# Hybrid encoder: token factors from the features-first input, and the pooled branch kept features-first

## The reference

```python
def rmsnorm(x, g):
    xf = x.astype(jnp.float32)
    y = xf * lax.rsqrt(jnp.mean(xf * xf, axis=-1, keepdims=True) + EPS)
    return (y * g.astype(jnp.float32)).astype(x.dtype)
...
        h = rmsnorm(x, norm1_g[l])
        z = jnp.matmul(h, w_in[l])
        u = z[..., :o1]
        qk = jax.nn.silu(centred_dwconv(z[..., o1:o3], conv_w[l], conv_b[l]))
...
        y_pool = pool_mixer(u, pool_w[l], pool_scale[l]).astype(x.dtype)
        y_mlstm = mlstm_mixer(q, k, v, o, gates, gate_b[l], mh_norm_g[l]).astype(x.dtype)
        x = x + jnp.matmul(jnp.concatenate([y_pool, y_mlstm], axis=-1), w_out[l])
        x = x + expert_choice_ffn(rmsnorm(x, norm2_g[l]), w_router[l], w_gate[l], w_up[l], w_down[l])
    return rmsnorm(x, final_g)[:, N_META:]
```

## Time and profile before

| | |
|---|---|
| median of 3 runs | 1764.13 us (1763.55 to 1764.77) |
| profiled execution | 1767.92 us, span 1766.1 us |
| granted TensorE clock, mean | 0.995 |
| busy share of the span | PE 98%, ACT 22%, DVE 24%, POOL 17% |
| first stage (to the last gate rows) | about 75 us of the span |
| output stage, with the ranking | about 655 to 846 us |
| experts' stage | about 854 us to the end |

### The profile page before, as it was taken

The page is one execution under the profiler, slowest core; times in us unless marked ns, Lnnn a source line. Parts: engine busy times, 40 slices in busy tenths (PEclk is TensorE's granted clock), DMA queues, the critical chain, the costliest instruction groups (busy, mean ns, idle before and its releaser), DMA issues.

```text
span 1766.1 us, 25121 instructions
## 1 busy us (share of the span) xinstructions
PE 1735.0 (98%) x10359; PEld 1403.2 (79%) x10359; DVE 420.5 (24%) x987; ACT 383.8 (22%) x890; POOL 298.4 (17%) x330
## 2 busy tenths in 40 slices
PE   9999999999999999999999999999999999999996
PEld 5556556855555774555899999999999999999996
DVE  4562113621020560069201101011010110101105
ACT  3335224332131533455000000000000000000005
POOL 0080022520101253443000010100101001010010
PEclk9999999999999999999999999999999999999998
DMA  9211012321110535534577676876859758587585
GB/s 297 78 51 52 20 36 76 90 89 36 36 39 18 163 101 182 177 99 154 197 251 278 214 250 232 294 250 211 279 205 310 261 187 283 212 307 255 181 278 227
DMA packets 178721, 307.28 MB, mean 174 GB/s; under 512 B 11068, under 2 KB 63468, under 8 KB 178528
## 3 DMA queue, kind: packets, MB, share of 16 engines
q1 hardware_dynamic: 171408, 283.30, 46.5%
q0 software_dynamic: 7248, 23.09, 5.2%
HBM read 275.02 MB, written 31.35 MB: 173 GB/s over the span
## 4 chain that ended last, share of the span: by engine, by line
PE 95%; ACT 1%; DVE 1%; DMA 1%; issue 1%; SPq 0%; POOL 0%; DVEq 0%; ACTq 0%; POOLq 0%
PE bank L2118 32%; PE bank L2138 16%; PE bank L1890 12%; PE bank L1867 9%; PE bank L2019 8%; PE bank L1801 3%; PE bank L1837 2%; PE bank L1953 2%; PE bank L1934 1%; PE bank L1849 1%; PE bank L1846 1%; PE bank L1845 1%; PE bank L2162 1%; PE bank L2093 1%; PE bank L1972 1%; PE bank L1943 1%
## 5 line engine op out<-in xcount | busy, mean ns | idle before, releaser
L2118 PE MATMUL bank<-arena 128*128 128x164 f32 x4096 | 579.7, 303 | 0.3 <-DVE arena L1658 0.3
L2118 PEld LDWEIGHTS bank<-arena 128*128 128x128 f32 x4096 | 571.8, 190 | 0.5 <-DVE arena L1658 0.5
L2138 PE MATMUL bank<-arena 128*128 128x164 f32 x2048 | 296.4, 303 | 0.4 <-DVE arena L1669 0.4
L2138 PEld LDWEIGHTS bank<-arena 128*128 128x128 f32 x2048 | 286.7, 190 | 0.6 <-DVE arena L1669 0.6
L1890 PE MATMUL bank<-arena 128*128 128x512 f32 (+1 forms) x576 | 214.0, 534 | 0.0
L1890 PEld LDWEIGHTS bank<-arena 128*128 128x128 f32 x576 | 110.0, 191 | 102.5 <-issue 92.7
L1669 DVE TENSOR_TENSOR arena<-bank,arena 128x328 f32<-128x328 f32 x64 | 32.0, 500 | 655.8 <-ACT arena L1241 655.8
L821 POOL DMA_INDIRECT residual<-arena,cur_scatter x30 | 44.9, 1497 | 691.3 <-DVE arena L1678 633.8
L1867 PE MATMUL bank<-arena 128*128 128x384 f32 x480 | 155.7, 485 | 0.0
L1241 ACT ACTIVATE arena<-bank 128x328 f32<-128x328 f32 x64 | 28.4, 443 | 558.5 <-PE bank L2118 558.5
L2019 PE MATMUL bank<-arena 128*128 128x512 f32 x320 | 146.0, 599 | 0.8 <-issue 0.8
(11 more groups left out here) (273 smaller groups left out, 1504.2 us busy)
## 6 DMA issues: line engine op xcount, KB each, us to landing
arena<-in_w_up SPq DMA_DIRECT2D x32, 2048.0 KB, 14.7
arena<-in_w_down SPq DMA_DIRECT2D x32, 2048.0 KB, 10.3
arena<-in_w_gate SPq DMA_DIRECT2D x32, 2048.0 KB, 8.3
arena<-in_w_in SPq DMA_DIRECT2D x7, 1536.0 KB, 6.5
arena<-in_x_sample SPq DMA_DIRECT2D x14, 512.0 KB, 5.9
arena<-x_features_first SPq DMA_DIRECT2D x11, 512.0 KB, 7.8
arena<-decay_rows SPq DMA_DIRECT2D x22, 256.0 KB, 4.6
arena<-state_rows SPq DMA_DIRECT2D x44, 128.0 KB, 4.0
```

What stands on the lines that cost most here:

```text
L2118: last = pe.matmul(ps[2 * w + fp % 2][:, a * SLOTS:(a + 1) * SLOTS], ring[2 * (fp // 2) + w][:, k, f * P:(f + 1) * P], xeT[:, k, SIDE[side ...
L2138: last = pe.matmul(to, ring[4 + dp // 2][:, k, dt * P:(dt + 1) * P], hidT[:, k, :], start=k == 0, stop=k == KT - 1)
```

## The change

It has two parts.

**Token factors.** The rows are no longer loaded in the first stage. ScalarE squares the whole tile of features (1024 columns, into `sq`). For the first tile TensorE adds up over features and blocks with eight products with ones. For the ten others GpSimd first adds the eight blocks in three steps of 512, 256 and 128 columns, and TensorE does one product with ones. ScalarE takes the root of the mean of all 128 by 128 values from the bank (`factor`, in `arena`), VectorE the reciprocal of all of them, and its eight products then read both the features and the factor from SBUF, each raising `h_ready` by itself. TensorE waits block by block for the first two tiles of `output_gate`, and for all eight blocks of a tile from the third on.

**Pooled branch.** The pooled product is formed features first, stored as `pool_features`, and loaded per tile by a new `load_pool` (256 features by 128 tokens) into the first 256 columns of `y_t`. Those two blocks need no transpose; `project` reads them directly. Several groups of `warm` are shorter or gone.

```diff
-        xin = [area("kT", D, shift=(1 + i) * D) for i in range(3)] + [area("qT", D, shift=i * D) for i in range(2)]
-        xin += [area("Cb", D, shift=i * D) for i in range(6)]
         ones = area("kT", P)
-        diag = [area("kT", P, shift=(1 + s) * P) for s in range(2)]
+        factor = [area("kT", P, shift=(1 + s) * P) for s in range(2)]
+        sq = [area("kT", D, shift=(1 + s) * D) for s in range(2)]
...
-            sp.dma_start(y_t[n % 2], y_d[i * P:(i + 1) * P, :]).then_inc(y_in[n % 2], 16)
+            sp.dma_start(y_t[n % 2][:, D_POOL:Y_W], y_d[i * P:(i + 1) * P, :]).then_inc(y_in[n % 2], 16)
+
+        def load_pool(sp, n):
+
+            if n >= 2:
+                multiplied(sp, ("wo", n - 2, 1))
+            pooled = y_t[n % 2][:, 0:D_POOL].rearrange("p (j t) -> p j t", j=2)
+            sp.dma_start(pooled, pool_d.rearrange("(j p) t -> p j t", p=P)[:, :, tile_cols(ORDER_B[n])]).then_inc(y_in[n % 2], 16)
...
-                    for p0, src in x_rows[i]:
-                        sp.dma_start(xin[i][p0:p0 + src.shape[0], :], src).then_inc(x_in[i], 16)
                     sp.dma_start(hT[:, :, tile_cols(i)], x_flipped.rearrange("p (k t) -> p k t", k=KT)[:, :, tile_cols(i)]).then_inc(tile_in[i], 16)
...
                         load_y(sp, n + 2)
                         load_x3(sp, n + 2)
+                        load_pool(sp, n + 2)
...
+                for i in range(1, NT):
+                    pool.wait_ge(sq_done, i + 1)
+                    for w in (512, 256):
+                        st.do(pool.tensor_tensor(sq[i % 2][:, 0:w], sq[i % 2][:, 0:w], sq[i % 2][:, w:2 * w], ALU.add))
+                        st.settle()
+                    pool.tensor_tensor(sq[i % 2][:, 0:P], sq[i % 2][:, 0:P], sq[i % 2][:, P:2 * P], ALU.add).then_inc(sum_ready, 1)
...
-                    act.wait_ge(x_in[tile], 16 * len(x_rows[tile]))
-                    st.settle()
-                    st.do(act.activation(area("scratch", D), xin[tile], ACT.Square, accum_out=small[:, i:i + 1]))
-                    st.settle()
-                    act.activation(small[:, 32 + i:33 + i], small[:, i:i + 1], ACT.Sqrt, scale=1.0 / D, bias=small[:, 94:95]).then_inc(sq_done, 1)
+                    act.wait_ge(tile_in[tile], 16)
+                    act.activation(sq[i % 2].rearrange("p (k t) -> p k t", k=KT), hT[:, :, tile_cols(tile)], ACT.Square).then_inc(sq_done, 1)
                     if i > 1:
                         take_o(i - 2)
+                        act.wait_ge(h_ready, KT * (i - 1))
+                    multiplied(act, ("x", i))
+                    b = plan[("x", i)][0]
+                    act.activation(factor[i % 2], ps[b][:, 0:P], ACT.Sqrt, scale=1.0 / D, bias=small[:, 94:95]).then_inc(free[b], 1)
...
-                    dve.tensor_scalar(diag[i % 2], ident[:, :], small[:, 48 + i:49 + i], None, ALU.mult).then_inc(diag_ready, 1)
...
-                        st.do(dve.scalar_tensor_tensor(h, h, g1c[:, k:k + 1], ps[b][:, 0:P], ALU.mult, ALU.mult))
...
+                    st.do(dve.reciprocal(factor[i % 2], factor[i % 2]))
...
+                        dve.scalar_tensor_tensor(h, h, g1c[:, k:k + 1], factor[i % 2], ALU.mult, ALU.mult).then_inc(h_ready, 1)
...
-                    pe.wait_ge(diag_ready, i + 1)
                     b = bank(("x", i))
-                    pe.matmul(ps[b][:, 0:P], ones, diag[i % 2], start=True, stop=True).then_inc(full[b], 1)
+                    if i == 0:
+                        pe.wait_ge(zeroed, 1)
+                        pe.wait_ge(sq_done, 1)
+                        for k in range(KT):
+                            last = pe.matmul(ps[b][:, 0:P], ones, sq[0][:, k * P:(k + 1) * P], start=k == 0, stop=k == KT - 1)
+                    else:
+                        pe.wait_ge(sum_ready, i)
+                        last = pe.matmul(ps[b][:, 0:P], ones, sq[i % 2][:, 0:P], start=True, stop=True)
+                    last.then_inc(full[b], 1)
...
-                    pe.wait_ge(h_ready, i + 1)
+                    if i > 1:
+                        pe.wait_ge(h_ready, KT * (i + 1))
...
-                                    for a in range(4 * g, min(4 * g + 4, NT)):
-                                        c = (a - 4 * g) * P
-                                        last = pe.matmul(ps[b][:, c:c + P], src[:, tile_cols(a)], pw[:, j, :], start=True, stop=True)
-                                    last.then_inc(full[b], 1)
+                                    lo, hi = 512 * g, min(512 * g + 512, T)
+                                    pe.matmul(ps[b][:, 0:hi - lo], pw[:, j, :], src[:, lo:hi], start=True, stop=True).then_inc(full[b], 1)
...
-                        for k in range(4):
+                        for k in range(D_POOL // P if name == "yT" and h == 0 else 0, 4):
                             last = pe.transpose(ps[b][:, k * P:(k + 1) * P], source(4 * h + k), ident[:, :])
...
-                    pe.wait_ge(y_in[n % 2], 16 * (n // 2 + 1))
+                    pe.wait_ge(y_in[n % 2], 32 * (n // 2 + 1))
```

More of the change, by code:

```diff
@@ L1102, in _, with move @@
                         last_norm(p)
-                def move(key, out, parts=P, w=512):
+                def move(key, out, parts=P, w=512, at=0):
                     multiplied(act, key)
-                    act.activation(out, ps[plan[key][0]][0:parts, 0:w], ACT.Copy).then_inc(free[plan[key][0]], 1)
+                    act.activation(out, ps[plan[key][0]][0:parts, at:w], ACT.Copy).then_inc(free[plan[key][0]], 1)
                 def halves(name, n, slots):
                     for h in range(2):
-                        move((name, n, h), slots[n % 2][:, 512 * h:512 * h + 512])
+                        lo = D_POOL if name == "yT" and h == 0 else 512 * h
+                        move((name, n, h), slots[n % 2][:, lo:512 * h + 512], at=lo - 512 * h)
                 def exponentials(part):
@@ L1826, in _ @@
                 gate_rows(NT - 2)
-                warm(3, 5)
                 gate_rows(NT - 1)
@@ L1870, in gate_columns @@
                 def gate_columns():
-                    warm(6, 5)
                     pe.wait_ge(rows_ready, 1)
```

46 lines of the change are left out of this document (18 added, 28 removed).

## The result

| | median | runs | profiled execution | span | mean granted clock |
|---|---|---|---|---|---|
| before | 1764.45 us | 1763.55 to 1767.82 (4) | 1767.92 | 1766.1 | 0.995 |
| changed | 1789.2 us | 1787.16 to 1792.05 (4) | 1789.83 | 1788.0 | 0.992 |

The changed kernel is slower: ratio 1.0133, 95% interval 1.012 to 1.0146. The medians differ by 24.75, the two profiled executions by 21.9. The forecast was 1778.5 with a range up to 1784, so the side was right and the size was not.

The account below looks back on a forecast made before the run. TensorE was taken as the bound, 95% of the chain. Start, eight-tile chain, transposes and pooled load summed as 1764.1 - 0.5 + 11.5 - 1.7 + 5.1 = 1778.5 us; range 1768 to 1784, by its own bounds 1775 to 1784.

Parts of the forecast that it names:

- the meeting on SBUF: First stage: GpSimd's three additions push themselves between VectorE's eight scalings, both in SBUF; stall of 1.3 to 1.9 per tile.
- the late load: Output stage: tile 9's pooled load, issued at about 790.86, lands at about 795.3, after TensorE wants it: +4.7.
- the start of the stage: First stage's start: fewer bytes ahead of the weights, more work for the first tile; -0.5, bounds -1.2 and +0.3.
- the chain of eight tiles: First stage, tiles 2 to 9: root, reciprocal and stretched scalings delay output_gate; 8 x 1.44 = +11.5, bounds 10.4 to 15.2.
- the transposes: Output stage: two transposes saved per tile, 0.22 each; -1.7 for tiles 0 to 7.
- Together +5.1: Output stage: late pooled loads, +4.7 at tile 9 and +0.6 at tile 10, less 0.22 for transposes; lower bound +3.2.
- Costed at nothing: Removed warm-ups stand where TensorE waits for ScalarE anyway; no cost taken, any effect would be through the clock.
- its last rival: The remainder: a slower time from something else, such as the lower clock level; chance 0.03.
- GpSimd shut out while VectorE's scalings run: First stage: GpSimd gets in only before the first scaling, wait before the factor product; 1772.4, chance 0.20.
- No disturbance: First stage: the engines don't disturb each other, chain of 3.8 hidden, tile 9's load still late; 1767.0, chance 0.12.
- Pooled tiles in time: Output stage: pooled loads come in time as well, only gains stand; 1761.9 down to 1760.5, chance 0.08.

Follow-up runs that it names:

- Experiment 3: Changed kernel without GpSimd's three additions per tile, so factors cover 128 of 1024 features: 1774.18 us, ratio 1.0045 to the kernel before.
- experiment 2: Changed kernel with the factor kept in its PSUM bank, so scalings read one operand from the bank: 1776.3 us, ratio 1.0052 to the kernel before.
- experiment 1: Changed kernel with the pooled load issued before the residual load: 1781.24 us, ratio 1.0083 to the kernel before.
- Experiment 4: Changed kernel with 22 products that nobody reads before TensorE's wait for tile 9's mixer output: 1796.64 us, ratio 1.017 to the kernel before.
- experiment 12: Kernel before with the pooled part alone, pooled load first, 12 increments and 24 more unread products in TensorE's gaps: 1762.89 us, ratio 0.9981.
- experiments 7: Changed kernel with factor in its bank, pooled load first and warm-ups put back: 1796.31 us, ratio 1.0162 to the kernel before.
- 8: Changed kernel with 22 unread products before tile 9's wait and the warm-ups put back: 1784.84 us, ratio 1.0104 to the kernel before.
- 10: Kernel before with the pooled part alone, pooled load first, and 108 semaphore increments heading TensorE's program: 1778.99 us, ratio 1.008.
- 11: Changed kernel with factor in bank, pooled load first, warm-ups back and 88 increments heading TensorE's program: 1780.1 us, ratio 1.0087 to the kernel before.
- 9: Changed kernel with 88 semaphore increments at the head of TensorE's program, no product added: 1811.05 us, ratio 1.0263 to the kernel before.
- Experiment 5: Changed kernel with the unread warm-up products put back to the old counts: 1811.6 us, ratio 1.0257 to the kernel before.

## Why the prediction was right or wrong, step by step

The forecast was a difference of 14.4 us; 24.75 was measured. The two causes that it counted on, the meeting on SBUF and the late load, are both there. By size, what it missed: the low clock behind tile 9's wait (3.0, a term that it did not have), the start of the stage (2.0), the chain of eight tiles (1.4, within its bounds), the low clock at the first experts' group (1.4), and the last tile's scalings (0.5), less 0.4 in the middle stages. Another 2.9 is how far the two profiled executions lay from their medians. The terms come to some 0.4 more than the whole, 10.4. The forecast's own upper bounds add up to 1783.0, not the 1784 that it gives, which changes nothing here.

**Right: the chain of a tile from the fourth on.** Root 0.38 (0.40 taken), reciprocal 0.95 (0.96), and the scalings stretched by GpSimd's additions. The tile's extra time is 1.61 where 1.44 was taken and 1.3 to 1.9 allowed; over eight tiles 12.9 instead of 11.5. It has two parts, and the sum knew only the first, TensorE's idle time, which was even a little less than taken:

```profile
28.05 1.61 PE L1812 MATMUL bank<-arena 128*128 128x400 f32 x4 [1.35 <-DVE arena L1361]
```

The other 0.26 is that the two blocks right behind the wait take 1.61 in the chain, where without a wait they took 1.35. The scalings grow by 1.84, the additions' full 2.5 less 0.7. Experiment 3 shows that VectorE's form is free without GpSimd, experiment 2 that the pair is free once one operand comes from a bank. The Trainium skill, SBUF — State Buffer, "Who interferes with whom", agrees on both points: an instruction with one SBUF input is outside the lock.

**Failed: the start of the stage, "I take -0.5".** It was +1.5 at the third factor product (22.05 instead of 20.51). The sum costed the scalings there as if GpSimd were silent, though the same additions meet tile 1's scalings: 4.00 at 19.07. From the second factor product to the third it takes 4.93 (4.86 in experiment 1) where experiment 3 takes 3.74, so the meeting costs 1.1 to 1.2 there. The rest of the miss is how late the second tile's features landed, which differs from one execution to the next: with the same first stage, experiments 1 and 4 are only 0.6 and 0.9 behind the kernel before, not 1.5. Without the meeting the start is where it was forecast, 20.07 and 19.98 in experiments 2 and 3, 0.4 and 0.5 under before. The last tile that meets additions, whose scalings took 4.47, adds 0.5. Up to u the meeting costs 14.1 to 15.3 (89.06 to 89.99 in three kernels that have it, 74.74 and 74.93 without), and the whole stage was +14.8 in the profiled execution instead of +11.0.

**Right: the transposes.** 1.7 by tile 8.

**Failed in its size: tile 9, "Together +5.1".** The wait itself is as forecast, 5.08 at tile 9 and 0.70 at tile 10. But the sum took the work behind the gap at the durations of before. It ran at the lower clock level, and cost 3 more: 3.25 and 3.29 instead of 1.75 and 1.96. Experiment 4 has the same wait without the idle time and no low clock, experiment 1 has neither. Together 8.1 instead of 5.1; experiment 1 gives back 7.1 of it between the first `project` and the first experts' group. This is the largest single miss: the prediction named the lower clock level in the warm-ups' term and in its last rival, and not behind the one long wait that it forecast.

**Failed: "Costed at nothing", the warm-ups.** The text said that if their cover mattered it would be through the clock, and put no number on it. Around the first keys the six kernels without the four products there lose 1.7 in five cases (granted clock below 1.00 between 280 and 315), the eight with them in none. The same gap in front of the second keys (1.17 at 574) is covered in experiment 12 alone; of the thirteen other kernels five lose 1.7 there, the profiled execution of before among them. So in the two profiled executions the one loss hides the other. A third place is before the gate columns, where six products went: the idle time there grew from 0.23 to 1.56, and the clock fell in all six kernels without them (1.7 in the changed one), but also in five of the eight with them, that of before again among them. That execution of before lies 3.5 above its median and that of the changed kernel 0.6 above, which is the difference between 21.9 and 24.75; the gap before the second keys accounts for 1.7 of it. At the first experts' group the loss (1.0 to 2.3) appears with the old counts as well (experiments 7, 8, 10 and 11) and is absent with the new ones in experiments 3, 4 and 9. In these three the clock fell all the same, 9 us earlier, on 22 products that nobody reads, which take 6.6 to 6.8 instead of 5.18. Experiment 4:

```profile
862.68 0.45 PE L2049 MATMUL bank<-ident,arena 16*128 16x16 f32 x4 [2.06 <-DVE arena L1651]
863.07 6.62 PE L2013 MATMUL bank<-ident 128*128 128x128 f32 x44
```

The idle time in front of the ranked rows is 2.05 with the new counts and 1.37 with the old ones, and the clock fell here or at the first group in all six kernels with the new counts, and in four of the seven with the old ones (in experiment 12, with still more products, it didn't). So the three products less make the fall likelier and are not its only cause; which execution meets it is open. Experiment 5's reading of it was too simple.

The sum redone with what was measured: 14.8 - 0.4 (middle) - 1.7 + 8.1 + 1.4 = 22.2 against 21.9.

**The rivals.** GpSimd shut out while VectorE's scalings run: no, the additions keep their length, and TensorE's idle time before the factor product is 0.9, once. No disturbance: no. Pooled tiles in time: no.

## What to carry to other kernels

A wait on TensorE has two prices: its own length, and what the work behind it takes at the lower clock level; here 5.1 and 3. When a helper's operand moves from a bank to SBUF, look for what GpSimd does at that moment, for the first tiles too. And when products are added or removed ahead of a loop, read the packets of the instruction queue before believing the time: 22 products that nobody reads (88 instructions) cost 10 us elsewhere.

## What the runs showed of the hardware

**The place of a loop in the program has a price.** Nine kernels fetch 43 packets (0.70 MB) on that queue and spend 901.7 from the second group on; five fetch 97 (1.59 MB) and spend 10 to 27 more. Counted in TensorE's programs (a product is four instructions, two matmuls with their weight loads; a transpose is two, an increment one), the loop stands 0, 205 or 216 instructions behind its place in the changed kernel in those without pauses, and 88, 97 or 128 in those with. With 128 there are two pauses in each of six iterations, some 3.6 together, with 88 one of 1.5. Both kernels of this comparison have no pause, so it is no part of their difference. The Trainium skill, Runtime: NRT & Kernel Launch, "Instruction fetch mechanics", says that instructions stream in blocks of 16 KB and that a jump to a target outside what is held must fetch it first; the packets' size (0.70 MB / 43) agrees, and here nine came anew at each jump back, not only the target's.

**A semaphore increment on TensorE took 0.15 to 0.16 us**: behind 88 of them, from the span's start, its first product is at 14.25, behind 108 at 17.29.

**VectorE's reciprocal goes by the column**: 0.178 for 4 columns, 0.292 for 22 and 0.95 for 128, where a scaling of the same size takes 0.27.

**Idle times as short as 1.2 us can be followed by the lower clock level.** The changed kernel before its first keys (TensorE, then windows):

```profile
293.38 1.53 PE L1778 MATMUL bank<-arena 128*32 128x96 f32 x64
296.08 0.85 PE L1864 MATMUL bank<-ident,arena 128*128 128x128 f32 x6 [1.17 <-issue]
...
299.31 0.85 PE L1864 MATMUL bank<-ident,arena 128*128 128x128 f32 x3
```

```profile
290.00:305.00 15.00, 13.33 (x120) 8.47 (x118) 3.29 (x9) 6.93 (x22) 2.15 (x2) 0.89 0.42 109
```

Six of these instructions take 0.85 and, three us later, three of them do. The same gap isn't followed by it in every execution (above).
